# Gate and up products of both experts of a pair in four column tiles of 32 tokens, in the second layer's mixture of experts

## The reference

```python
cap = EC_FACTOR * n // N_EXPERTS          # 2 * 256 // 16 = 32 tokens an expert
g, idx = lax.top_k(jnp.swapaxes(aff, 1, 2), cap)
xs = jax.vmap(lambda hb, ib: hb[ib])(h, idx)
hid = jax.nn.silu(jnp.einsum('becd,edf->becf', xs, w_gate)) * jnp.einsum('becd,edf->becf', xs, w_up)
y = jnp.einsum('becf,efd->becd', hid, w_down) * g[..., None].astype(h.dtype)
return jax.vmap(lambda yb, ib: jnp.zeros((n, d), h.dtype).at[ib.reshape(-1)].add(yb.reshape(-1, d)))(y, idx)
```

## Time and profile before

| | |
|---|---|
| runs shown | 3071.65, 3075.71, 3076.5 us |
| profiled execution, its own time | 3077.43 us |
| its span, first to last instruction | 3075.8 us |
| PE busy | 2755.1 us (90%) |
| DVE, ACT, POOL busy | 1298.0, 898.2, 195.9 us |
| mean granted clock of PE | 0.941 |
| DMA, whole span | 527.36 MB, mean 171 GB/s |
| experts of layer 1, first product to last down product | 2833.81 to 3059.10 us of the span |
| DMA in 2850 to 3040 us | share 1.01, 428 GB/s |

### The profile page before, as it was taken

One profiled execution on the slowest core, in us unless ns is written; L12 is line 12 of the kernel. 1 busy time (PEld: TensorE's weight loads), 2 busy tenths in 40 slices (PEclk: granted clock), 3 DMA queues, 4 the chain that ended last, 5 costly groups with the idle time before them and its releaser, 6 DMA issues. The chain is left out here.

```text
span 3075.8 us, 42149 instructions
## 1 busy us (share of the span) xinstructions
PE 2755.1 (90%) x15242; PEld 1933.2 (63%) x15242; DVE 1298.0 (42%) x2168; ACT 898.2 (29%) x1437; POOL 195.9 (6%) x341
## 2 busy tenths in 40 slices
PE   5999998998899998999998878997985989787998
PEld 4777775666677776777776557994663433564333
DVE  4333355444533335433336655665534233552112
ACT  2222225443422223322124433444322100532000
POOL 0110002320010110110100001000000000000000
PEclk9999998998899999999998988998997999888999
DMA  7755332323374652563743226652103899414996
GB/s 257 237 185 155 107 96 63 76 67 91 119 226 143 202 180 86 178 222 113 231 149 84 63 62 224 178 160 77 35 7 137 335 427 413 106 42 179 428 428 290
DMA packets 428522, 527.36 MB, mean 171 GB/s; under 512 B 29718, under 2 KB 382484, under 8 KB 415988
## 3 DMA queue, kind: packets, MB, share of 16 engines
q1 hardware_dynamic: 392884, 399.54, 37.6%
q0 software_dynamic: 35520, 126.24, 12.8%
HBM read 524.68 MB, written 1.05 MB: 171 GB/s over the span
## 5 line engine op out<-in xcount | busy, mean ns | idle before, releaser
L1747 DVE TENSOR_TENSOR wlo<-raw,whi 128x1024 fp32r<-128x1024 f32 x392 | 478.2, 1223 | 491.8 <-ACT whi L1316 467.1
L1316 ACT ACTIVATE whi<-raw 128x1024 fp32r<-128x1024 f32 x392 | 413.6, 1057 | 642.1 <-PE bank L673 584.3
L671 PE MATMUL bank<-xhi,whi 128*128 128x512 f32 (+1 forms) x1568 | 580.2, 370 | 3.1 <-DVE xlo L2260 3.1
L672 PE MATMUL bank<-xlo,whi 128*128 128x512 f32 (+1 forms) x1568 | 565.4, 361 | 0.0
L673 PE MATMUL bank<-xhi,wlo 128*128 128x512 f32 (+1 forms) x1568 | 563.2, 359 | 0.0
L671 PEld LDWEIGHTS bank<-xhi,whi 128*128 128x128 f32 x1568 | 296.6, 189 | 95.8 <-issue 53.4
L673 PEld LDWEIGHTS bank<-xhi,wlo 128*128 128x128 f32 x1568 | 297.1, 189 | 46.5
L672 PEld LDWEIGHTS bank<-xlo,whi 128*128 128x128 f32 x1568 | 297.1, 189 | 41.1 <-issue 0.7
L671 PE MATMUL bank<-hhi,whi 128*128 128x512 f32 (+1 forms) x704 | 261.1, 371 | 21.3 <-DVE hlo L1854 21.3
L672 PE MATMUL bank<-hlo,whi 128*128 128x512 f32 (+1 forms) x704 | 260.3, 370 | 0.0
L673 PE MATMUL bank<-hhi,wlo 128*128 128x512 f32 (+1 forms) x704 | 259.8, 369 | 0.0
(11 more groups left out here) (284 smaller groups left out, 3298.3 us busy)
## 6 DMA issues: line engine op xcount, KB each, us to landing
raw<-in_ffn_w_in SPq DMA_DIRECT2D x176, 512.0 KB, 4.3
mod_ring<-in_w_mod POOLq DMA_DIRECT2D x128, 512.0 KB, 4.3
experts<-in_w_gate SPq DMA_DIRECT2D x32, 2048.0 KB, 16.4
experts<-in_w_up SPq DMA_DIRECT2D x32, 2048.0 KB, 20.9
experts<-in_w_down SPq DMA_DIRECT2D x32, 2048.0 KB, 16.8
mod_ring<-in_w_ada POOLq DMA_DIRECT2D x96, 512.0 KB, 4.7
raw<-in_ffn_w_out SPq DMA_DIRECT2D x64, 384.0 KB, 3.2
raw<-in_ffn_w_out SPq DMA_DIRECT2D x64, 320.0 KB, 3.0
```

The source lines that it names most:

```text
L671: pe.matmul(o, wh, hi[:, k0 + k, cols], start=(first and k == 0), stop=False)
L672: pe.matmul(o, wh, lo[:, k0 + k, cols], start=False, stop=False)
L1316: act.activation(whi[:, slot, :], raw[:, slot, :], ACT.Copy).then_inc(*n.mark("hi_ready"))
L1747: dve.tensor_tensor(wlo[:, slot, :], raw[:, slot, :], whi[:, slot, :].bitcast(F32), ALU.subtract)\
```

## The change

In layer 1 a new `both_gate_up(p)` takes the place of `gate_up(p, 0)` and `gate_up(p, 1)`. It first acquires both banks and waits for all four gate and up units of the pair, then runs 8 steps of four matmuls: gate 0 on partitions 0 to 31 and up 0 on 64 to 95 of bank 0, gate 1 on 32 to 63 and up 1 on 96 to 127 of bank 1. The four rounds of `combine(p - 1)` follow it in one piece. ACT and DVE wait once for both experts and read the new partitions; SP's list of loads and the ring stay as they are, but the counts that free the four gate and up slots are now those of the joint product. Layer 0 is not touched.

```diff
--- before.py
+++ after.py
@@ -444,7 +444,7 @@
         def expert_used(l, u):
 
             p, (kind, i) = u // len(PAIR_UNITS), PAIR_UNITS[u % len(PAIR_UNITS)]
-            done = l * N_EXP + 2 * p + i + 1
+            done = l * N_EXP + 2 * p + (i + 1 if l < DEPTH - 1 else 2)
             if kind == "gate":
                 return [(s["gate_used"], done)]
             if kind == "up":
@@ -1224,6 +1224,22 @@
                             if j == KD - 1:
                                 mm.then_inc(s[done], 1)
 
+                def both_gate_up(p):
+
+                    tiles = []
+                    for i in range(2):
+                        acquire(i)
+                        for part, kind in enumerate(("gate", "up")):
+                            pe.wait_ge(*expert_full(l, p, (kind, i)))
+                            at0 = part * HD + i * CAP
+                            tiles.append((bank[i][at0:at0 + CAP, :], i, experts[expert_slot(p, (kind, i))[1]], ("gate_used", "up_used")[part]))
+                    for j in range(KD):
+                        for to, i, w, done in tiles:
+                            mm = pe.matmul(to, xsT[:, j, 2 * p + i, 0:CAP], w[:, j * 512:(j + 1) * 512],
+                                           start=(j == 0), stop=(j == KD - 1), skip_group_check=True)
+                            if j == KD - 1:
+                                mm.then_inc(s[done], 1)
+
                 def turn():
 
                     pe.wait_ge(*n.next("hid_ready", 2))
@@ -1268,8 +1284,11 @@
                                     mm.then_inc(s[f"bank_ready{b}"], 1)
 
                 for p in range(PAIRS):
+                    if not ctx_too:
+                        both_gate_up(p)
                     for i in range(2):
-                        gate_up(p, i)
+                        if ctx_too:
+                            gate_up(p, i)
                         if p:
                             combine(p - 1, (2 * i, 2 * i + 1))
                     turn()
@@ -1703,9 +1722,11 @@
                 table_of(ACT.Silu)
                 for p in range(PAIRS):
                     for i in range(2):
-                        act.wait_ge(*n.next("gate_used"))
-                        act.wait_ge(*n.next("up_used"))
-                        act.activation(sg[i * HD:i * HD + ns, :], bank[i][0:ns, :], ACT.Silu).then_inc(*n.mark("silu_ready"))
+                        if ctx_too or i == 0:
+                            act.wait_ge(*n.next("gate_used", 1 if ctx_too else 2))
+                            act.wait_ge(*n.next("up_used", 1 if ctx_too else 2))
+                        at0 = 0 if ctx_too else i * CAP
+                        act.activation(sg[i * HD:i * HD + ns, :], bank[i][at0:at0 + ns, :], ACT.Silu).then_inc(*n.mark("silu_ready"))
                         n.next(f"bank_read{i}")
                         if p:
                             combined((2 * i, 2 * i + 1))
@@ -2337,9 +2358,11 @@
                 for p in range(PAIRS):
                     for i in range(2):
                         dve.wait_ge(*n.next("silu_ready"))
-                        dve.wait_ge(*n.next("up_used"))
+                        if ctx_too or i == 0:
+                            dve.wait_ge(*n.next("up_used", 1 if ctx_too else 2))
                         own()
-                        dve.tensor_tensor(hid[i * HD:i * HD + ns, :], sg[i * HD:i * HD + ns, :], bank[i][HD:HD + ns, :], ALU.mult)\
+                        at0 = HD if ctx_too else HD + i * CAP
+                        dve.tensor_tensor(hid[i * HD:i * HD + ns, :], sg[i * HD:i * HD + ns, :], bank[i][at0:at0 + ns, :], ALU.mult)\
                             .then_inc(*n.mark(f"bank_read{i}"))
                         own()
                         dve.sem_inc(*n.mark("hid_ready"))
```

## The result

The changed kernel takes 3097.91 us (median of 6 runs, 3089.94 to 3102.38), the kernel before 3073.21 us in 6 runs: ratio 1.0079, 95% interval 1.0062 to 1.0096. It is slower, as forecast; the forecast of 3093.5 us is 0.14% low and the time lies in the stated range. The profiled execution took 3093.96 us, its span is 3092.3 us. One of the seven runs of experiment 6's kernel with eight slots took 4690.19 us at a mean clock of 0.553; its median counts that run, its ratio leaves it out.

What follows compares the result with a forecast made beforehand. Layer 1's experts were taken as bound by their weights. +13.2 us to the last T, +1.7 and +2.7 behind it make +17.6 on 3077.4, 3095 us; less 1.7 for the median, 3093.5 us, own range 3088 to 3099.

Steps and rivals of the forecast that it cites:

- What bounds the layer: Layer 1's experts are bound by their weights: six units a pair, 29.4 us at 428 GB/s, with PE's work shorter.
- Four tiles side by side: Joint gate and up product: four different streams run together, 7.06 us at full clock, replacing two products of 7.06 us each.
- First pair gains nothing: Layer 1's first pair: first refill issued as before, now four units at once; the queue was already full, so no gain.
- T: The landing of a pair's second up matrix in layer 1, before which no matmul of the joint product starts.
- The queue: Weight loads between pairs: queue dry or nearly so at T + 8.9, refill takes 22.9 us; 31.8 us a pair against 29.4.
- The clock: PE, idle some 10 us a pair, starts each joint product behind the first at half clock: 8.76 us instead of 7.06.
- Behind the last T: End of layer 1: last joint product +1.7 us at half clock, longer combine chain to `turn` +2.7 us.
- The sum: Whole kernel: +13.2 us up to the last T, +1.7 and +2.7 us behind it, in sum +17.6 us.
- the cover: Rival, chance 0.15: between T and the refill, two queued down units bridge the product; not slower, 3077 to 3081.5 us.
- the tiles: Rival, chance 0.05: the joint product's four tiles don't go fully side by side, 9 to 14 us each; 3107 to 3142 us.
- the third: Rival, chance 0.12: in layer 1's pairs the refill's start is dearer or the slow clock lasts longer; 3100 to 3107 us.

Runs made afterwards that it cites:

- experiment 6: Kernel before with seven weight slots in layer 1 instead of six: 3067.65 us, ratio 0.9972 to the kernel before; with eight slots: 3064.61 us, ratio 0.9966.
- experiment 1: Changed kernel with nine extra matmuls, result unused, behind each layer 1 pair's down product except the last: 3088.66 us, ratio 1.0040 to the kernel before.
- experiment 4: Changed kernel with seven weight slots in layer 1 instead of six: 3075.36 us, ratio 0.9997 to the kernel before.
- experiment 2: Changed kernel with five extra matmuls, result unused, behind each layer 1 pair's down product except the last: 3088.95 us, ratio 1.0046 to the kernel before.

## Why the prediction was right, and where its sizes were off

- **What bounds the layer**: right. A ring with one slot more takes away the loss between the pairs while the products stay as slow, and takes time off the kernel before.
- **Four tiles side by side, 7.06 us at full clock**: right, 7.07 us in experiment 1 with four different streams.
- **First pair gains nothing, first T**: right. 2857.16 - 2834.36 = 22.8 us behind the first refill, 22.9 forecast.
- **The queue**: right, including its size. The dip begins about 8 us behind T, a microsecond earlier than forecast, so the queue had run dry and was not merely about to. From the first of four issues to the fourth landing it is 22.7 to 23.6 us in the six pairs, 23.0 in the mean, 22.9 forecast. The 2.0 us a DMA that the prediction set beside this from the Trainium skill ("DMA: Bandwidth & Descriptors", Anatomy of one DMA) stand there for DMAs issued from GpSimd, and these are issued from SP. The sum did not use them.
- **The clock**: right in kind, mis-sized, and this is the term that failed in size. I took 8.76 us for the product, from the single row of a short wait. The six products that set the refills took 8.85, 9.91, 8.86, 9.97, 8.79 and 9.89 us, 9.4 in the mean. That is 0.6 us a pair, 3.7 us of the 4.4 by which the sum up to the last T was low (+17.6 us measured, from 3052.60 - 2834.36 against 3041.55 - 2840.87; +13.2 forecast). Every second product is the long one. The long ones come after a down product of 9.7 to 9.8 us and 7.0 us of idle; the short ones behind the first pair's come after a down product of 7.06 us and 9.8 to 10 us of idle. Why the two alternate was not tried, and the seven-slot kernel of experiment 4 has no such order (9.98 and 8.86 us both follow a down product of 7.06 us).
- **Behind the last T**: `turn` begins 13.3 us behind it, 4.2 us later than before, 4.4 forecast (1.35 us of product, 2.9 us of combine). Here is the end of it in the timeline of DVE:

```profile
3062.86 1.85 DVE L2355 SCALAR_TENSOR_TENSOR h<-bank,mod,h 128x256 f32<-128x256 f32 x4 [0.21 <-DVEq L2368]
...
3064.82 0.69 DVE L2365 TENSOR_TENSOR hid<-sg,bank 32x512 f32<-32x512 f32 x1
```

  As forecast, `hid` of the second expert stands behind the adding of two rounds. What I left out is that the down product behind would also be at half clock: 9.45 us instead of 7.06. Combine behind it was faster in turn (4.17 against 5.63 us), and from `turn` to the store it is 22.0 us against 20.75, +1.25 us.
- **The sum**: 17.6 + 4.2 + 1.25 = 23.0 us in the stretch, 17.6 forecast. The median is in the forecast's own range of 3088 to 3099 us, which was wide enough for two terms that were too small, the product at half clock and the work behind the last T. (By the prediction's own terms the sum is 3075.7 + 17.6 = 3093.3 us, 0.2 us under the forecast.)
- **The rivals**: the cover did not hold (share 0.93, clock 0.50 at the start of each product); the tiles did go side by side; of the third, the slow clock did last longer than in the one row, while the start was not dearer.

What each part costs, by the runs: 29.6 us a pair in a full queue, 30.0 to 31.3 us with a product at full clock and the queue drained, 32.6 us with the clock as it is. So of the 3.0 us that a pair loses, some 2.3 go by the clock (9.4 against 7.07 us of product), and the rest to the late issue itself. That split is an estimate: no run had the clock at 1.00 in every pair, no product held up and every refill at 23 us. Between the pairs neither costs anything once the queue has a unit more to work on; behind the last T the cost stays.

## What to carry to other kernels

Where a ring of buffers feeds a stage that DMA bounds, a faster product was worth nothing here, and merging two products costs what the merged wait takes from the queue: count the bytes still queued when the product starts, and compare them with the time until its slots are issued again, at the slow clock. If one more buffer can be found, it hides both between the transfers, and filled ahead of the stage it also shortens the stream. Then give the same buffer to the kernel before and compare again: here that one was the faster. Behind the last transfer the order of the work counts again: what is moved from a wait to there is paid in full.

## What the runs showed of the hardware

- A refill issued before the unit ahead of it had landed did not save its start: in experiment 1 the issue at 2867.88, 2.8 us ahead of that landing, had its fourth unit land 22.8 us later, and three others 2.5 to 3.0 us ahead took 23.7 to 24.1 us, where four units at the full queue's 4.9 us are 19.6 us.
- After 7 to 11 us of idle the half clock cost a product between 1.3 and 2.9 us (8.41 to 9.97 us against 7.07 at full clock), in a range that one row could not show. In experiment 2 it cost 1.4 to 2.8 us after 4.4 to 6.2 us of idle. Idle of 2.2 to 2.4 us cost nothing there, while 2.17 us before the product of 2942.66 in the kernel before had cost it 1.7 us.
- The half clock came back within a pair: after a product that had ended at clock 1.00 and a combine with gaps of 0.7 us, the down product of 2872.48 took 9.78 us with the clock at 0.50 from 2872 to 2877 us, against 7.06 us at 2905.32 behind gaps of the same length.
